# The order of the matmuls inside a weight chunk: bank after bank, or product after product

## The reference

```python
qa, ka, va, qb, kb, vb, ga, gb = in_proj(x, w_in)        # one projection, split by columns
oa = banded_attention(qa, ka, va, ...)                   # sliding window 128, sinks
ob = combine_dilations(...)                              # three dilated windows
mix = (sigmoid(ga) * (oa @ w_oa) + sigmoid(gb) * (ob @ w_ob)) @ w_out
h = layer_norm(ALPHA * x + mix, ln1_g, ln1_b)
gate, up = split(h @ w_ffn_in, 2)
y = layer_norm(ALPHA * h + (silu(gate) * up) @ w_ffn_out, ln2_g, ln2_b)
```

## Time and profile before

| what | value |
|---|---|
| time, median of 3 runs | 1822.49 us (1819.56 to 1826.4) |
| profiled execution, first to last instruction | 1823.3 us (its whole time is not listed apart) |
| TensorE, matmuls busy | 1747.2 us (96%), 12451 instructions |
| TensorE, weight loads busy | 1660.6 us (91%), 12451 instructions |
| VectorE busy | 995.4 us (55%) |
| ScalarE busy | 725.3 us (40%) |
| GpSimd busy | 156.4 us (9%) |
| mean granted TensorE clock | 0.972 of full speed |

### The profile page before, as it was taken

One profiled execution on the slowest core, in us unless ns is written; L12 is line 12 of the kernel. 1 busy time (PEld: TensorE's weight loads), 2 busy tenths in 40 slices (PEclk: granted clock), 3 DMA queues, 4 the chain that ended last, 5 costly groups with the idle time before them and its releaser, 6 DMA issues.

```text
span 1823.3 us, 32494 instructions
## 1 busy us (share of the span) xinstructions
PE 1747.2 (96%) x12451; PEld 1660.6 (91%) x12451; DVE 995.4 (55%) x1389; ACT 725.3 (40%) x1054; POOL 156.4 (9%) x257
## 2 busy tenths in 40 slices
PE   8999999998999998999959999999999999999995
PEld 7999999766989896999959999999999999999995
DVE  4457667554377575666664444444444444444546
ACT  4343443353433232334344544443333333333333
POOL 1012222323010100000050000000000000000001
PEclk9999999897999998999979999999999999999997
DMA  6579999668688887677837878876775555556541
GB/s 217 155 267 315 324 321 342 164 180 256 223 301 298 306 290 233 220 228 252 254 128 237 256 246 265 250 230 213 259 224 165 167 161 161 165 167 200 163 155 52
DMA packets 204717, 410.75 MB, mean 225 GB/s; under 512 B 12220, under 2 KB 105686, under 8 KB 200416
## 3 DMA queue, kind: packets, MB, share of 16 engines
q1 hardware_dynamic: 178384, 254.41, 43.7%
q10 hardware_dynamic: 7488, 91.33, 15.0%
q0 software_dynamic: 18768, 63.94, 10.8%
HBM read 403.47 MB, written 94.92 MB: 273 GB/s over the span
## 4 chain that ended last, share of the span: by engine, by line
PE 77%; DVE 8%; DMA 7%; issue 4%; ACT 2%; POOL 1%; DVEq 0%; SPq 0%; ACTq 0%
PE bank L1289 74%; DMA VST<-in_cache_b_dram 3%; PE bank L1292 3%; DMA raw<-in_w_in_dram 3%; DVE wlo L898 1%; DVE PV L1091 1%; DVE PV L1094 1%; POOL U L572 1%; ACT L859 1%; DVE U L1205 1%; DVE U L1195 1%; DVE VST L1082 1%; ACT whi L615 0%; DMA xs_s<-in_x_sample_dram 0%; DVE VST L1085 0%
## 5 line engine op out<-in xcount | busy, mean ns | idle before, releaser
L898 DVE TENSOR_TENSOR wlo<-raw,whi 128x1024 fp32r<-128x1024 f32 x473 | 576.1, 1226 | 646.9 <-ACT whi L615 646.3
L615 ACT ACTIVATE whi<-raw 128x1024 fp32r<-128x1024 f32 x473 | 498.2, 1060 | 837.6 <-PE bank L1289 611.0
L1289 PE MATMUL bank<-X1H,whi 128*128 128x288 f32 x1408 | 420.1, 298 | 17.6 <-DVE X1L L1212 11.7
L1289 PE MATMUL bank<-X1L,whi 128*128 128x288 f32 x1408 | 417.4, 296 | 0.0
L1289 PE MATMUL bank<-X1H,wlo 128*128 128x288 f32 x1408 | 415.8, 295 | 0.0
L1289 PE MATMUL bank<-XH,whi 128*128 128x288 f32 x1248 | 375.1, 301 | 0.7 <-issue 0.5
L1289 PE MATMUL bank<-XL,whi 128*128 128x288 f32 x1248 | 369.9, 296 | 0.0
L1289 PE MATMUL bank<-XH,wlo 128*128 128x288 f32 x1248 | 368.6, 295 | 0.0
L1289 PEld LDWEIGHTS bank<-X1H,whi 128*128 128x128 f32 x1408 | 265.7, 189 | 21.5 <-issue 16.8
L1289 PEld LDWEIGHTS bank<-X1H,wlo 128*128 128x128 f32 x1408 | 267.0, 190 | 0.0
L1289 PEld LDWEIGHTS bank<-X1L,whi 128*128 128x128 f32 x1408 | 266.1, 189 | 0.0
(11 more groups left out here) (234 smaller groups left out, 1789.7 us busy)
## 6 DMA issues: line engine op xcount, KB each, us to landing
raw<-in_w_ffn_in_dram SPq DMA_DIRECT2D x176, 512.0 KB, 3.6
raw<-in_w_in_dram SPq DMA_DIRECT2D x156, 512.0 KB, 6.0
out_dram<-in_cache_b_dram ACTq DMA_DIRECT2D x28, 2336.0 KB, 10.9
raw<-in_w_ffn_out_dram SPq DMA_DIRECT2D x88, 512.0 KB, 4.1
KST<-in_cache_b_dram POOLq DMA_DIRECT2D x32, 512.0 KB, 5.1
QST<-tok_scratch POOLq DMA_DIRECT2D x32, 512.0 KB, 6.6
VST<-in_cache_b_dram POOLq DMA_DIRECT2D x16, 1024.0 KB, 12.9
raw<-in_w_out_dram SPq DMA_DIRECT2D x32, 512.0 KB, 5.3
```

The lines of the kernel that those rows point to most:

```text
L615: nc.scalar.activation(whi[s][:, :], raw[s][:, :], ACT.Copy).then_inc(hi_done, 1)
L898: nc.vector.tensor_tensor(wlo[s][:, :], raw[s][:, :], whi[s][:, :].bitcast(F32), ALU.subtract).then_inc(lo_done, 1)
L1289: return nc.tensor.matmul(out, lhsT, rhs, start=start, stop=stop, **kw)
```

## The change

In every chunk but a group's last, the loops change places: the row block is outermost, then the three products, and the output tile innermost, so that neighbouring matmuls write different banks (four in turn with `m_n=4`, two with `m_n=2`). `free_wait(m)` stands as before ahead of the first product into bank m. The last chunk of a group keeps its order, and so does the announcing of its tiles. Each bank still receives the same products in the same order.

```diff
                 w = CK // kk
-                for m in range(m_n):
+                for q in range(0 if last else kk):
+                    for weights, moving in ((whi, hi), (whi, lo), (wlo, hi)):
+                        for m in range(m_n):
+                            st = first and q == 0 and weights is whi and moving is hi
+                            if st and free_wait:
+                                free_wait(m)
+                            ins = mm(bank[banks + m][:, 0:T], weights[s][:, q * w + m * P:q * w + m * P + P],
+                                     moving[:, k0 + q, :], st, False)
+                for m in range(m_n if last else 0):
                     if first and free_wait:
                         free_wait(m)
                     for q in range(kk):
```

## The result

The changed kernel takes 1841.9 us (median of 4 runs, 1838.28 to 1845.79) against 1821.31 us (4 runs): a ratio of 1.0102, with a 95% interval of 1.0078 to 1.0125, so about 1% slower. The two medians lie 20.6 us apart. The forecast was 1840, in a range from 1833 to 1850. The profiled execution has a span of 1843.7 us (before: 1823.3) and a mean granted clock of 0.972, as before.

What follows compares the result with a forecast made beforehand. TensorE's matmul line was taken to bound the kernel almost everywhere (74% of the span). Group-start waits of 6.0 + 6.0 + 1.8 + 2.4 + 1.1 + 0.45 = 17.7 us, added to the 1822.49 us median, gave 1840, range 1833 to 1850.

Steps and rivals of the forecast that it cites:

- The mechanism and its place: Waits at a group's first chunk: banks are needed earlier, so TensorE waits on read-outs; 17.7 us in sum.
- Rival C: Group starts: something else equally late absorbs the stalls, as in PH_GATE; 1822 to 1831 us; chance 0.08.
- PH_OUT and PH_F2's second half, 6.0 us each: Three group starts in each: VectorE's sums between read-outs free bank 3 late, 2.0 us lost per start.
- PH_F1's first half 2.4, PH_F2's first half 1.8, PH_F1's second half 1.1, PH_QA 0.45: Group starts: 10 at 0.24 us, 3 at 0.6, 11 at 0.1 (bounds 0 and 1.1), and one at 0.45.
- PH_MERGE nothing: PH_MERGE's group start: read-outs end at 743.55, the bank is wanted at 749.05, so no loss.
- PH_GATE nothing, 3.3 without its cover: Seven group starts 0.47 us late, taken as zero because TensorE idles 4.92 us for VectorE's PV at stage end.
- Order inside a chunk, zero within +-6 us: 392 turned chunks: some 8100 more bank changes cost nothing, since two stages with different change rates have equal pace.
- the prediction's own sign: TensorE's pace within a group stays 133.3 ns; another pace makes the prediction wrong at its root.
- Rival B: Every turned product: alternating banks gives back time lost writing one bank twice running; up to 125 us, 1715; chance 0.05.
- The 122.5 ns: Product spacing estimated from the Trainium skill's warm formula N/2.4 + 2.5, leaving 10.8 ns per product unexplained.
- The clock, no fall: Six stalls in PH_OUT and PH_F2's second half: no fall of the granted clock; the other end six, 8 us.
- Rival A: PH_OUT and PH_F2's second half: half clock after each long stall, 1.4 us each, 1848 us; chance 0.13.

Runs made afterwards that it cites:

- (f): Kernel before, changed only in chunks neither first nor last: products in a row into one bank as before, but row blocks alternating between neighbours; 1822.3 us in one run.

## Why the prediction was right, and where it was off

- *The mechanism and its place.* Right, and shown: the new order in the first chunks alone costs the whole loss, start by start as forecast (the table there), and without them nothing is lost. Rival C, stalls that something else absorbs, did not come true.
- *PH_OUT and PH_F2's second half, 6.0 us each.* The stalls are as forecast: 2.0 us a start, most of it made by the sums. PH_F2's second half grew by 5.2 (6.0 less the faster spacing). PH_OUT grew by 8.0: two falls of the clock came on top, which the sum had left out.
- *PH_F1's first half 2.4, PH_F2's first half 1.8, PH_F1's second half 1.1, PH_QA 0.45.* The third product of PH_F1's group came 0.60 us after the first, the fifth of PH_F2's 1.14 after its first, as worked out. The three stages grew by 1.6, 1.0 and 0.0 us. That is about 0.8 us less than forecast in the first two, which is what the faster spacing gives back there. In the third a start cost 0.06 us, some 0.7 in all and not 1.1, and the spacing took the rest.
- *PH_MERGE nothing.* No new wait there. The stage took 1.0 us less, 78.0 us; in the other profiles it takes 78.1 to 79.0.
- *PH_GATE nothing, 3.3 without its cover.* The starts are late by 0.47 us, as forecast (537.67). The sign that had been named, an idle time before PH_MERGE that shrinks by 3.3, did not come: it was 5.07 us. So the reason given for zero, a PV chain that does not depend on these starts, is not borne out: in the 14 profiles the stage's last weight product comes 238.1 to 242.4 us after its first, and VectorE's last PV instruction ends 4.3 to 5.7 us behind it each time. The cover moves with TensorE. How much of the 3.3 us reaches the end stays open; neither the time nor the stage's scatter tells.
- *Order inside a chunk, zero within +-6 us.* This term was mis-sized: it is a gain of some 6 to 7 us by the estimate above, of which the middle chunks alone show 4.7 in the time. By the prediction's own sign, a pace other than 133.3 ns, it was wrong at its root here: the pace was 132.5 and 132.8. The reasoning from two paces of 133.33 at two rates of bank changes held as far as it went: it shows that a bank change alone costs nothing in the old order of operands, but the new order also changes which operands are neighbours, and that was not weighed. Rival B, a gain from alternating, had the sign right, at 0.5 to 0.8 ns a product, but turning the banks is not enough for it. The 122.5 ns named beside it come from a formula with no term for a weight load, and every product here has one; the fastest groups here ran at 130.0 ns.
- *The clock, no fall.* Mis-sized too: two falls in the profile of the changed kernel, some 2.8 us, where six would have been 8. Rival A took place in part. In the three profiles with the long stalls of both stages (the changed kernel, the first-chunk one and the one with PH_GATE old) 6 of 18 such starts were followed by half clock.

The faster spacing (6 to 7 us less) and the falls of the clock (2.8 more) have opposite signs. Another 5.1 us of the profiles' difference lie ahead of PH_MERGE: 3.1 in PH_GATE, and 2.0 before it, a stretch that takes 465.7 to 475.4 us in the 14 profiles. That the sum came within 3 us of the measured difference is therefore in part luck.

What the Trainium skill reports of another kernel's bank cycling and the clock ("TensorE: Matmul & The Clock Gate", section "A second HAM failure mode: psum-queue depth-cycling"), small idle pieces between groups and a clock that swings, agrees with the traces only so far: the clock did fall after stalls for banks (839.40, 897.40), and after four other such stalls of the same profile it did not. Within PH_F1's groups, where banks turn at every product of most chunks, it stayed at 1.00 for the 240 us of this window of the changed kernel:

```profile
1395.00:1635.00 240.00, 240.00 (x1804) 1.00 0.53 164
```

## What to carry to other kernels

When accumulation banks are turned inside a chunk, every bank of the next group is wanted at once, while the group before gives them back one at a time: compare the end of each bank's read-out with the moment of its first write, before and after, and the loss can be read from one trace. Keep the first chunk of a group bank after bank; where it cannot be, let nothing stand between the read-outs. A steady pace that does not move with one property of the order does not prove that it moves with none.

## What the runs showed of the hardware

- Matmuls of 288 columns with a weight load each run at 133.33 ns in three orders that keep the bank; in others at 132.5, 131.6 or 130.0, at the same full clock. One order (f) had 130.0 in two of PH_OUT's groups and 133.3 in the other two. Where the row blocks alternate, their sequence and not the banks goes with the pace.
- After a wait for VectorE's read-out the waiting product starts 0.05 to 0.06 us behind its end, and the next ungated one 0.24 us after that (PH_OUT, 838.94 and the start after it).
- Stalls of 2 us in pieces of about 1.1 us, parted by single products, were followed by 3.4 us of half clock (1.2 GHz) in 6 cases of 18; with the stall cut to some 0.6 us there was none after six starts, and in the old order none after 60.
